# Two transformer blocks on one core: the expert phase as one block, rows one by one on VectorE, context products of TensorE in loops

## What is computed

```python
def peer_ffn(h, w_pq, sub_keys, peer_u, peer_v):
    ...                                   # 8 heads choose 16 of 16384 experts for every token
    gates = jax.nn.softmax(top, axis=-1)
    u = peer_u[ib]                        # 128 rows of 1024 numbers for each token
    act = jax.nn.gelu(jnp.einsum('btd,bthkd->bthk', hb, u), approximate=False)
    return jnp.einsum('bthk,bthkd->btd', gb * act, peer_v[ib])

def ffn_sublayer(x, mod, k, g_pre, g_post, w_gu, w_down):      # w_gu 1024 x 5632, w_down 2816 x 1024
    h = rmsnorm(x, g_pre) * (1 + mod[k + 1]) + mod[k]
    gu = h @ w_gu
    y = (jax.nn.silu(gu[..., :D_FF]) * gu[..., D_FF:]) @ w_down
    return x + 0.5 * mod[k + 2] * rmsnorm(y, g_post)

def short_conv_mixer(h, w_in, w_conv, w_out):                  # w_in 1024 x 3072, w_out 1024 x 1024
    b, cg, u = split(h @ w_in, 3)
    up = pad(cg * u)
    return (b * (w_conv[0] * up[:-2] + w_conv[1] * up[1:-1] + w_conv[2] * up[2:])) @ w_out
```

## Time and profile before

| | |
|---|---|
| median of 3 runs | 4243.65 us |
| profiled execution, its time | 4238.47 us |
| profiled execution, its span | 4236.7 us |
| TensorE busy | 2721.9 us (64%) |
| VectorE busy | 2673.1 us (63%) |
| ScalarE busy | 982.5 us (23%) |
| GpSimd busy | 961.8 us (23%), all of it row fetches |
| traffic | 1034.40 MB, mean 244 GB/s |
| of it rows (queue 0) and weights (queue 1) | 536.94 MB, 495.51 MB |

### The profile page before, as it was taken

The page is one execution under the profiler, slowest core; times in us unless marked ns, Lnnn a source line. Parts: engine busy times, 40 slices in busy tenths (PEclk is TensorE's granted clock), DMA queues, the critical chain, the costliest instruction groups (busy, mean ns, idle before and its releaser), DMA issues. The chain is left out here.

```text
span 4236.7 us, 44741 instructions
## 1 busy us (share of the span) xinstructions
PE 2721.9 (64%) x16804; PEld 2359.7 (56%) x16804; DVE 2673.1 (63%) x3884; ACT 982.5 (23%) x1358; POOL 961.8 (23%) x1028
## 2 busy tenths in 40 slices
PE   6776649937389308676569610000798698977698
PEld 5555428835178307475258610000798598975498
DVE  3635686674777795544966778998645555545554
ACT  2333210010110003332110000000444344533343
POOL 0000024452454540000044556665000000000000
PEclk8978769967699759787679855555899799988899
DMA  6543679997799974432789999998344244541153
GB/s 236 192 160 108 243 310 381 412 374 278 288 390 412 378 296 161 169 128 98 314 310 413 394 347 358 367 377 327 130 158 156 103 160 149 166 144 44 40 186 112
DMA packets 229372, 1034.40 MB, mean 244 GB/s; under 512 B 29657, under 2 KB 32617, under 8 KB 180073
## 3 DMA queue, kind: packets, MB, share of 16 engines
q0 software_dynamic: 147456, 536.94, 32.7%
q1 hardware_dynamic: 81768, 495.51, 32.3%
HBM read 1031.30 MB, written 1.05 MB: 244 GB/s over the span
## 5 line engine op out<-in xcount | busy, mean ns | idle before, releaser
L270 DVE TENSOR_TENSOR w_lo<-raw,w_hi 128x1024 fp32r<-128x1024 f32 (+1 forms) x492 | 558.6, 1138 | 700.2 <-ACT w_hi L257 699.7
L1740 POOL DMA_INDIRECT arena_layer<-in_peer_u,arena_layer x512 | 481.3, 940 | 1632.6 <-SPq L833 1165.8
L1788 DVE SCALAR_TENSOR_TENSOR ps<-arena_layer,ps 128x1024 f32<-128x1024 f32 x512 | 660.2, 1290 | 85.8 <-DMA arena_layer<-in_peer_v,arena_layer 50.8
L1792 DVE CUSTOM_DVE_ANT_0 arena_layer<-arena_layer,ps 128x1024 f32<-128x1024 f32 x512 | 608.8, 1219 | 147.4 <-DMA arena_layer<-in_peer_u,arena_layer 121.5
L628 PE MATMUL ps<-hT_hi,w_hi 128*128 128x256 f32 x2240 | 644.7, 288 | 70.7 <-PEq L763 31.6
L257 ACT ACTIVATE w_hi<-raw 128x1024 fp32r<-128x1024 f32 (+1 forms) x492 | 485.1, 989 | 796.3 <-PE ps L628 795.1
L628 PE MATMUL ps<-hT_lo,w_hi 128*128 128x256 f32 x2240 | 642.8, 287 | 0.0
L628 PE MATMUL ps<-hT_hi,w_lo 128*128 128x256 f32 x2240 | 642.2, 287 | 0.0
L628 PE MATMUL ps<-parts_context,raw 128*128 128x256 f32 x2496 | 568.3, 390 | 94.2 <-issue 78.6
L628 PEld LDWEIGHTS ps<-parts_context,raw 128*128 128x128 f32 x2496 | 487.4, 196 | 174.8 <-issue 106.6
L1740 POOL DMA_INDIRECT arena_layer<-in_peer_v,arena_layer x512 | 480.3, 938 | 351.5 <-DVE ps L1788 251.1
(11 more groups left out here) (361 smaller groups left out, 2957.4 us busy)
## 6 DMA issues: line engine op xcount, KB each, us to landing
raw<-in_ffn_w_gu SPq DMA_DIRECT2D x154, 1024.0 KB
raw<-in_w_mod SPq DMA_DIRECT2D x72, 1024.0 KB
raw<-in_w_ada SPq DMA_DIRECT2D x48, 1024.0 KB
raw<-in_w_in SPq DMA_DIRECT2D x44, 1024.0 KB
raw<-in_ffn_w_down SPq DMA_DIRECT2D x56, 768.0 KB
raw<-in_ffn_w_down SPq DMA_DIRECT2D x56, 640.0 KB
raw<-in_conv_w_in SPq DMA_DIRECT2D x24, 1024.0 KB
raw<-in_w_o SPq DMA_DIRECT2D x8, 1024.0 KB
```

The lines of the kernel that those rows point to most:

```text
L270: dve.tensor_tensor(self.lo[:, k, 0:n], self.raw_part(g, parity, k // 2, g.starts(k), g.starts(k + 1)), self.hi[:, k, 0:n].bitcast(F32), A ...
L1740: gp.indirect_dma_start(self.grow[:, slot % GR, :], None, self.tables[slot // half_way], bass.IndirectOffsetOnAxis(ap=self.index[:, k:k + ...
L1788: dve.scalar_tensor_tensor(out=self.tile, in0=row, scalar=cell, in1=self.tile, op0=ALU.mult, op1=ALU.add) \
L1792: dve.tensor_tensor_reduce(row, row, self.tile, 1.0, 0.0, ALU.mult, ALU.add, cell).then_inc(row_used.sem, 1)
```

## The change

The expert phase of a layer becomes one `nc.Block`. Between the context stages, TensorE, ScalarE and VectorE wait for each other's end of the stage (`stage_after`, `stage_ended`) and GpSimd and SP for nothing. GpSimd issues all 512 rows in one run. The ring has 16 buffers: 8 in the arena as before and 8 over `w_hi` and `w_lo`. VectorE's rows are written out one by one with constant waits (no loop), their numbers per stage are set freely: a feed-forward takes 12, 8 for each of the 11 tiles, 44 and 6; the convolution 12, 8 for each of 6 tiles (the first 32 ahead of any context work), 16 and 6, none at the taps. The copies of 16 cells in and out of `small` go; the dots are written to `acts` directly. In most stages VectorE signals its part done first and takes its rows behind that. The gelu is made in two parts on ScalarE, the gates multiplied when a value tile begins. TensorE's convolution in and down are loops. ScalarE copies the keys in layer 1.

```diff
+    more_rows = nc.alloc_sbuf_tensor_at("expert_rows", [P, 8, D], F32, offset=split_base)
-    GR = 8
+    GR = 16
+    def stage_after(eng, *others):
+        for other in others:
+            eng.wait_ge(other.sem, other.base)
+    def stage_ended():
+        for signal_ in (context_pe, context_act, context_dve):
+            signal_.base += 1
...
+        def fetch(self, block):
+            @block.gpsimd
+            def _(gp):
+                for n in range(ROWS):
+                    gp.wait_ge(row_used.sem, row_used.at(n + 1))
+                    k = n % (TT * SLOTS)
+                    gp.indirect_dma_start(
+                        self.grow[n % GR], None, self.tables[n // (TT * SLOTS)],
+                        bass.IndirectOffsetOnAxis(ap=self.index[:, k:k + 1], axis=0)) \
+                      .then_inc(row_landed[n % GR].sem, 16)
...
+        def rows(self, dve, n):
+            for q in range(self.next, self.next + n):
+                values, k = q // (TT * SLOTS), q % (TT * SLOTS)
+                if q % SLOTS == 0:
+                    (self.enter_values if values else self.enter_features)(dve, k // SLOTS)
+                dve.wait_ge(row_landed[q % GR].sem, row_landed[q % GR].at(16 * (q // GR + 1)))
+                row, cell = self.grow[q % GR], self.acts[:, k:k + 1]
+                if values:
+                    dve.wait_ge(row_used.sem, row_used.at(GR + q))
                     dve.scalar_tensor_tensor(out=self.tile, in0=row, scalar=cell,
                                              in1=self.tile, op0=ALU.mult, op1=ALU.add) \
                        .then_inc(row_used.sem, 1)
                 else:
                     dve.tensor_tensor_reduce(row, row, self.tile, 1.0, 0.0,
                                              ALU.mult, ALU.add, cell).then_inc(row_used.sem, 1)
...
-    def down(name, hff, experts=None, heads=0, row=None):
+    def context_down(block, name, hff, row, experts, n_rows):
+            stage_after(pe, context_act, context_dve)
+            gate_row(pe)
+            with pe.Fori(0, 2) as i:
+                for q in range(4):
+                    u, half = q // 2, q % 2
+                    if half == 0:
+                        unit_wait(pe, u, i)
+                    project_tokens(pe, i * 4 + q, tiles_of(u, width), parts, half * 11,
+                                   opens=(half == 0), closes=(half == 1),
+                                   j=half, turn=i * 2 + u)
+            pe.drain().then_inc(context_pe.sem, 1)
...
+        @block.vector
+        def _(dve):
+            stage_after(dve, context_pe, context_act)
+            gate_columns(dve, *row)
+            dve.drain().then_inc(context_dve.sem, 1)
+            experts.rows(dve, n_rows)
...
+    def context_conv_in(block, h, b_gate, u, up, experts, n_rows):
+            in_pairs(6, pe, tile)
+            pe.drain().then_inc(context_pe.sem, 1)
...
+            experts.rows(dve, 4 * n_rows)
+            stage_after(dve, context_pe, context_act)
+            v.tick(dve.memset(up[:, :, 0:1], 0.0))
+            v.tick(dve.memset(up[:, :, SEQ + 1:SEQ + 2], 0.0))
+            for t in (4, 5):
+                experts.rows(dve, n_rows)
+                product_wait(dve, t)
...
-        if l == 0:
-            context_ffn("z00", 0, 0, 0, experts, (1, 5, 3, 1))
-            context_conv(experts)
-            context_ffn("z01", 0, 6, 4, experts, (1, 5, 3, 1))
-        else:
-            context_ffn("z10", 1, 0, 0, experts, (1, 5, 3, 1))
-            ...
-            experts.alone(HEADS // 2 - experts.done)
-            experts.weigh()
-        experts.alone(HEADS - experts.done)
+        with nc.Block(no_gpsimd_drain=True) as block:
+            experts.fetch(block)
+            if l == 0:
+                context_ffn(block, "z00", 0, 0, 0, experts, (12, 8, 44, 6))
+                experts.activate(block, 0)
+                context_conv(block, experts, (12, 8, 16, 6))
+                context_ffn(block, "z01", 0, 6, 4, experts, (12, 8, 44, 6), 1)
+            else:
+                context_ffn(block, "z10", 1, 0, 0, experts, (12, 8, 44, 6))
+                h, kz = carve((KC, SEQ), (TT, 2 * NKV, HD), of=parts)
+                context_norm_in(block, 1, 3, 2, h, experts, 12)
+                context_keys(block, h, kz, context_v[:], context_kT[:], experts, 12)
+                experts.activate(block, 0)
+                experts.activate(block, 1)
+            experts.rest(block, ROWS)
```

More of the change, by code:

```diff
@@ L1763, in use @@
[L1763 to L1787 removed]
+            self.next = 0
@@ L1835, in end, with rest, _ @@
-        def end(self):
-            assert self.done == HEADS
-            row_used.base += HEADS * TOPK
-            dots_kept.base += HEADS
-            tile_in_psum.base += HEADS // PEER_HEADS + 1
-            for s_ in range(GR):
-                row_landed[s_].base += 16 * HEADS * TOPK // GR
-    def fetching(block, experts, heads):
-        if experts is not None:
-            @block.gpsimd
-            def _(gp):
-                experts.fetch(gp, heads)
+            self.next += n
+        def rest(self, block, upto):
+            @block.vector
+            def _(dve):
+                self.rows(dve, upto - self.next)
@@ L1850, in peer_end @@
+        def end(self):
+            assert self.next == ROWS
+            row_used.base += ROWS
+            gelu_made.base += TT
+            tile_in_psum.base += TT + 5
+            for s_ in row_landed:
+                s_.base += 16 * ROWS // GR
     def peer_end(l, y):
@@ new lines, in context_out, with _ @@
+    def context_out(block, name, h, row, experts, n_rows):
+        weights.begin(name)
+        @block.sync
+        def _(sp):
+            weights.feed(sp)
+        @block.tensor
+        def _(pe):
+            stage_after(pe, context_act, context_dve)
+            gate_row(pe)
+            for t in range(2):
+                unit_wait(pe, t, 0)
+                project_tokens(pe, t, tiles_of(t), (h,))
+            pe.drain().then_inc(context_pe.sem, 1)
+        @block.scalar
+        def _(act):
+            stage_after(act, context_pe, context_dve)
+            for t in range(2):
+                product_wait(act, t)
+                act.copy(y_tok[:, :, t * 512:(t + 1) * 512],
+                         ps[:, t, :].rearrange("p (t n) -> p t n", t=TT)).then_inc(unit_free[t].sem, 1)
+                squares(act, t, 512)
+            act.drain().then_inc(context_act.sem, 1)
+        @block.vector
+        def _(dve):
+            stage_after(dve, context_pe, context_act)
+            gate_columns(dve, *row)
+            dve.drain().then_inc(context_dve.sem, 1)
+            experts.rows(dve, n_rows)
+        stage_ended()
+        cols_ready.base += 1
+        pe_done.base += 1
+        units_used(2)
+        weights.end()
```

629 lines of the change are left out of this document (323 added, 306 removed).

## The result

The changed kernel took 4290.02 us (median of 20 runs, 4270.27 to 4301.52) beside 4244.64 for the kernel before: ratio 1.010, interval 1.0084 to 1.0116. It is slower; the forecast was 4168, and its range for 8 in 10 was 4110 to 4236.

What follows compares the result with a forecast made beforehand. Feed-forwards bound by transfers, the convolution by a chain of stages, remaining rows by VectorE's pace. Layer 0 -35 and layer 1 -41 us give -76: 4168 us from 4243.65, own range 4140 to 4200, 8 in 10 within 4110 to 4236.

Steps and rivals of the forecast that it cites:

- The step that failed: Argument against Rival C: down's written-out products ran at 412 GB/s without a gap, so saturated DMA engines need not lengthen gaps.
- -10 for the first feed-forwards: First feed-forward of each layer: 281 us instead of 291.1 in layer 0, as barriers go and the idle 2% mostly closes.
- Rival C: Unbroken fetches lengthen TensorE's gaps in convolution in, out and norm, and keys: 52 us lost, 4220 us; chance 0.16.
- Rival D: Written-out rows behind context work issue slowly, 0.65 us more per row hit; with 190 hit 4290 us; chance 0.10.
- Rival B: TensorE's gaps vanish because the loops leave none: convolution 23 us and features 7 us shorter still, 4138 us; chance 0.22.
- Convolution: Layer 0's convolution: norm 28, products 84, gaps 15, taps 12, out 40, add 9; 188 us against 250.6, -62.
- Second feed-forward: Layer 0, after the convolution: 10 fewer rows, 112.5 MB; 283 us instead of 302.8, -20.
- Rest: Layer 0's rows behind all context work: 130 and some 4 at 1.39 us, 189 us instead of 132, +57.
- Features: Layer 1's feature rows and keys' weights: 148 us instead of 178.3, -30, the least certain term.
- Values: Layer 1's 256 value rows written out at 1.39 us: 359 to 361 us instead of 361.1, -1.
- The signs: Forecast wrong if convolution exceeds 210 us or a rest row 1.45; gaps between every product beyond some 20 us mean Rival C.
- The loops: TensorE's down and convolution in: by a skill's rule, taken branches could cost 1 or 2 us a turn; the trace spoke against.

Runs made afterwards that it cites:

- ring_of_8: The changed kernel with 8 row buffers instead of 16, without those over `w_hi` and `w_lo`; ratio 0.9954 to the kernel before, with gaps.
- gated_all: The changed kernel with VectorE's rows of down and convolution in gated by TensorE's products; ratio 0.9818 to the kernel before, with gaps.
- before_again: The kernel before, unchanged, run once more for a trace on an occasion without gaps; its one execution took 4154.50 us.
- before_pe_loops: The kernel before with only TensorE's loops in convolution in and down; ratio 1.0019 to the kernel before, on an occasion with gaps.
- waits_in_fours: The changed kernel with only every fourth value row waiting for landings, for four at once; ratio 1.0049 to the kernel before, with gaps.

## Why the prediction was wrong

**The step that failed** is "Against: down made 352 written-out products in 76.14 us at 412 GB/s with no gap", with -10 for the first feed-forwards. I took saturated DMA engines for the condition, and found down proof against it. The condition, on an occasion with gaps, is a dense run of GpSimd's fetches. The stretch of 47.3 us from 808.5 us on has 23 fetches and 221 products before, 32 fetches (40 us of 47 at 1.25 us each) and 31 products now, at 412 and 409 GB/s. The two first feed-forwards came out 42 and 49 us longer, not 10 shorter: down has 30 us of gaps in each, the first pass of gate-up 14 more than before.

What makes the fetches denser in down is the ring of 16 together with 44 rows in one run. In the kernel before nothing in the code holds VectorE's rows of down back either, but with 8 buffers VectorE soon waits for landings, and GpSimd with it (VectorE is busy for 30.0 of the 47.3 us before, for 36.2 now). Either half alone keeps the first down whole: 8 buffers with ungated rows (`ring_of_8`, 352 products in 76.83 us), and 16 buffers with rows tied to TensorE's half tiles (`gated_all`, 76.75). Tied so in down and in convolution in, the kernel has a ratio of 0.982 where the changed one had 1.010. That a series feeds itself is a reading of one more number, not tested: inside it the weight queue is busy for 3.7% of the engines' time, 38.6% in the same stretch before, so nearly all of the bandwidth goes to rows and landings hold the fetching back least.

**Rival C** had the mechanism, rows without a break lengthening the gaps, with convolution in and the keys as its places and +52 us as its price. Measured: 104 us more of gaps, 61 of them in down, 28 in the first passes of gate-up, 11 in the keys and 5 in convolution in; 82 us more of time. It had stood at 4220. Rival D gave 4290, the measured number, by a mechanism that did not happen: value rows came at 1.39 us in both layers, not 1.9.

**Rival B** named what happens without gaps, 4138; there the changed kernel gains 28 us of span (30 by the medians) of 4155, not 106.

**Convolution** -62: measured -55 with 28 us of gaps and -44 without, where before had no gaps to lose: of its 250.6 us, 46 were the occasion's (204.6 in `before_again`). The sum of 188 against 195.4 is right in size by luck. By the traces norm took 16.7 us where the sum has 28, products in 123.7 (84 + 15), taps 13.5 (12), out 31.5 (40), add 10 (9): the gaps of convolution in cost 25 more than the sum gives them, and norm and out took that back.

**Second feed-forward** -20: -27 (108.6 MB moved, not 112.5), and -35 without gaps. **Rest** +57: +59.

**Features** -30: -16 and -15. Without gaps the stretch takes 150.0 us at 410 GB/s, the 148 of the sum; its bytes are 61.5 MB, not 66, so the bound of 160 was too high. The saving is half of what I took since the kernel before needs only 164.6 there, and with gaps (162.5 us, 373 GB/s) the keys have 11 us of them.

**Values** -1: -1 with gaps and +10.5 without. The kernel before has 12 us less there without gaps, its head boundaries not being late then; the 0.067 us for 256 rows, 17 us, was the right term.

**First feed-forwards without gaps**: -2 and +1 against -10 each: the kernel before runs them at 402 to 403 GB/s there, 392 to 393 in the earlier trace rows. What I took for idle time of barriers goes with the gaps. The 281 us itself was right there, 281.8 and 278.7.

So of -76, 48 were missing even without gaps (first feed-forwards 19, convolution 18, features 15, values 11, rest 2; the second feed-forward gave 15 more), and the gaps took 82. For much of the 48 the step is the base: the sum set stages of the changed kernel that fit an occasion without gaps against stages of the kernel before from one with them.

**The signs.** Neither of the two that would have called the forecast wrong came (convolution 195.4, not over 210; a rest row 191.3/134 = 1.43, not over 1.45): both looked away from the feed-forwards. The sign for C, gaps between every product beyond 20 us, did come.

**The loops** cost nothing that the runs show: the changed kernel has 0.9934 with them, 0.9939 and 0.9935 written out, all without gaps, and `before_pe_loops` 1.0019 (0.9971 to 1.0068) with gaps.

**Slips in the sums** that change nothing: faster adds up to 0.81 by the chances given, not 0.79; layer 1 moves 305 MB by its windows, not 309; the bounds given for the parts of layer 0 add up to -63 to +2, not -75 to +10.

**Open.** Why the gaps come on some occasions is not known. That what runs dry is the supply of instructions to the engine fits the even steps (in down's series the trace has a weight load and a product in turn, mostly 1.40 or 0.70 us apart), but no run shows when instructions were asked for. The transfers of the series 808.5 to 855.8 by queue hold a single packet of instructions (packets, MB, share of the engines' time):

```profile
q0 software_dynamic: 5115, 18.64, 98.8%
q1 hardware_dynamic: 169, 0.71, 3.7%
q14 instruction: 1, 0.01, 0.0%
```

Whether TensorE's loops matter in the changed kernel where gaps appear is open too: both runs of the written-out version fell on occasions without.

## What to carry to other kernels

When a ring of buffers is deepened and its users are given their work in one run, ask what paced the engine that fills it, and what it will do without that: here GpSimd's fetches, and through them TensorE. A long queue of indirect fetches issued back to back went, on the occasions with gaps, with another engine starved of issue even where bytes were to be had, so tie them to the progress of the engine that must not starve. And a difference of 1% between kernels can change its sign with the occasion: look at whether the same gaps stand in both traces before the ratio is believed, and before times of the one are taken as the base for the other.

## What the hardware showed that was not expected

- While GpSimd issues indirect fetches each 1.25 us, TensorE on some occasions gets its instructions in steps of 0.70 us (products 1.4, 2.1 or 2.80 us apart), at 187 GB/s as at 410. The medians of the kernel before went from 4155 to 4256 us with the occasion, and on one chip from 4155.4 to 4236.1.
- VectorE's sequencer has the same step: the 709 ns of the earlier trace rows fall on an occasion with gaps, and there layer 1's values took 361.1 us before; without gaps its longest such wait is 45 ns, and the values took 349.1.
- A second semaphore on a written-out value row costs 0.067 us, 5% of the row: 1.392 us from start to start with two waits, 1.325 with one, in `waits_in_fours` as in the loop before.
- Waiting for one landing in eight fetches, which looks free, costs 7% of the kernel, 277 us.
